# Prompt tiles 1 to 6 in pairs: attention tile by tile, the output stages of both on one stream of weights

## The reference

```
xn = rms_norm(x);  z = xn @ w_in                      # latents, retention q k v, gates
q  = rms_norm(q_lat) @ w_uq ;  q_abs = q_nope . w_uk
o_lat = softmax(q_abs . ckv + q_pe . krope) . ckv     # 8 heads, causal
o_ret = retention over chunks of 128 rows, 4 heads, state carried from chunk to chunk
o_a = (o_lat . w_uv) @ w_oa ;  o_b = (silu(rg) * group_norm(o_ret)) @ w_ob
x  += (sigmoid(ga) * o_a + sigmoid(gb) * o_b) @ w_out
xn2 = rms_norm(x) ;  q = xn2 @ peer_w_q               # 8 heads x 2 halves
s = q . sub_keys ; the best 16 of each half, then the best 16 of their sums: 128 experts a token
y = sum over the 128 experts e of  g_e * gelu(peer_u[e] . xn2) * peer_v[e]
out = rms_norm(x + y)
```

## Time and profile before

| | |
|---|---|
| runs | 4175.75, 4164.13, 4177.30 us |
| the profiled execution, its span | 4170.0 us (the profile gives no other time for it) |
| TensorE busy | 3270.2 us, 78% |
| VectorE busy | 2704.6 us, 65% |
| GpSimd busy | 2494.4 us, 60% |
| ScalarE busy | 739.7 us, 18% |
| 16 DMA engines | 1498.19 MB, mean 359 GB/s |
| mean granted TensorE clock | 0.912 of 2.4 GHz |

### The profile page before, as it was taken

How to read it: one execution, slowest core, us unless ns; L and a number is a source line. 1 busy time by engine, 2 the same in 40 slices (tenths; PEclk the granted TensorE clock), 3 DMA queues, 4 the chain that set the end, 5 groups by cost and what they waited for, 6 DMA issues and landing times.

```text
span 4170.0 us, 39232 instructions
## 1 busy us (share of the span) xinstructions
PE 3270.2 (78%) x11253; PEld 1605.8 (39%) x11253; DVE 2704.6 (65%) x6214; ACT 739.7 (18%) x2273; POOL 2494.4 (60%) x2069
## 2 busy tenths in 40 slices
PE   7877877767888877867988777877898777799854
PEld 3334333332344332423444333433353323466532
DVE  2156568766876578766876577657875686655544
ACT  2112111220112111211121022202131120211111
POOL 0005766777666767776666667666667675544452
PEclk9998999988999999889989999999999997899976
DMA  5668999999999999999999999999999999999996
GB/s 184 219 225 301 402 391 400 353 403 381 398 372 376 403 395 343 365 402 402 384 369 398 402 371 364 382 402 398 390 389 398 397 349 346 327 320 323 327 387 232
DMA packets 580362, 1498.19 MB, mean 359 GB/s; under 512 B 90506, under 2 KB 147475, under 8 KB 580147
## 3 DMA queue, kind: packets, MB, share of 16 engines
q0 software_dynamic: 297216, 1082.26, 67.8%
q1 hardware_dynamic: 242850, 401.10, 26.7%
q10 hardware_dynamic: 40082, 12.32, 1.2%
HBM read 1485.33 MB, written 10.13 MB: 359 GB/s over the span
## 4 chain that ended last, share of the span: by engine, by line
PE 35%; DMA 24%; POOL 16%; issue 11%; DVE 10%; ACT 3%; another core or an unknown queue 1%; ACTq 0%; SPq 0%; DVEq 0%; POOLq 0%
POOL rows L723 15%; DMA rows<-in_peer_v_dram,pe_id 14%; PE PS L1185 12%; PE PS L818 11%; DMA rows<-in_peer_u_dram,pe_id 4%; PE PS L1102 3%; DVE rows L2136 3%; PE PS L827 2%; DMA wbuf<-in_w_in_dram 2%; DMA wbuf<-in_peer_w_q_dram 2%; DMA wbuf<-in_w_out_dram 2%; PE PS L783 1%; DVE xr L2162 1%; PE PS L963 1%
## 5 line engine op out<-in xcount | busy, mean ns | idle before, releaser
L723 POOL DMA_INDIRECT rows<-in_peer_u_dram,pe_id x1024 | 1241.3, 1212 | 919.7 <-PE PS L1185 308.9
L1185 PE MATMUL PS<-rows,diags 128*128 128x512 f32 x2544 | 1357.0, 666 | 457.4 <-DMA rows<-in_peer_v_dram,pe_id 394.8
L723 POOL DMA_INDIRECT rows<-in_peer_v_dram,pe_id x1024 | 1233.8, 1205 | 697.0 <-DVE dots L2136 379.1
L2136 DVE CUSTOM_DVE_ANT_0 rows<-rows,px 128x1024 f32<-128x1024 f32 x1024 | 1242.2, 1223 | 503.0 <-DMA rows<-in_peer_u_dram,pe_id 477.7
L1185 PEld LDWEIGHTS PS<-rows,diags 128*128 128x128 f32 x2544 | 490.8, 208 | 1105.4 <-issue 987.6
L818 PE MATMUL PS<-wbuf,xt 128*128 128x512 f32 (+1 forms) x1696 | 781.1, 597 | 81.4 <-DMA wbuf<-in_w_in_dram 38.3
L2162 DVE SCALAR_TENSOR_TENSOR xr<-rows,gcoef,xr 128x1024 f32<-128x1024 f32 x388 | 498.4, 1285 | 158.9 <-issue 146.5
L818 PEld LDWEIGHTS PS<-wbuf,xt 128*128 128x128 f32 x1696 | 322.1, 197 | 510.4 <-issue 364.2
L818 PE MATMUL PS<-wbuf,wide 128*128 128x512 f32 (+1 forms) x736 | 344.8, 610 | 37.4 <-ACT wide L1292 15.2
L2242 ACT ACTIVATE diags<-ident,gcoef 128x128 f32<-128x128 f32 x636 | 231.1, 399 | 203.7 <-PE PS L1185 81.7
L818 PEld LDWEIGHTS PS<-wbuf,wide 128*128 128x128 f32 x736 | 145.1, 202 | 221.8 <-issue 163.2
(11 more groups left out here) (374 smaller groups left out, 2665.6 us busy)
## 6 DMA issues: line engine op xcount, KB each, us to landing
wbuf<-in_w_in_dram SPq DMA_DIRECT2D x278, 512.0 KB
wbuf<-in_peer_w_q_dram SPq DMA_DIRECT2D x136, 512.0 KB
wbuf<-in_w_out_dram SPq DMA_DIRECT2D x68, 512.0 KB
wbuf<-in_w_ob_dram SPq DMA_DIRECT2D x66, 512.0 KB
wbuf<-in_w_oa_dram SPq DMA_DIRECT2D x36, 512.0 KB
rows<-in_peer_u_dram,pe_id POOLq DMA_INDIRECT x1028, 4.3
rows<-in_peer_v_dram,pe_id POOLq DMA_INDIRECT x1024
KV<-in_cache_ckv_dram SPq DMA_DIRECT2D x128, 128.0 KB
```

The source lines that it names most:

```text
L723: pool.indirect_dma_start(row_slot(kind, n), None, a["peer_u" if kind == "u" else "peer_v"][0], bass.IndirectOffsetOnAxis(ap=pe_id[t % 2][ ...
L1185: last = nc.tensor.matmul(bank[3 + 4 * c], diag(n), row_slot("v", n)[:, c * 512:(c + 1) * 512], start=start, stop=stop)
L2136: V.tensor_tensor_reduce(out=row, in0=row, in1=px[:, :], scale=1.0, scalar=0.0, op0=ALU.mult, op1=ALU.add, accum_out=dots[:, at_:at_ + 1]) ...
```

## The change

The prompt's fronts become *units*: (0), (1, 2), (3, 4), (5, 6), (7). In a unit of two, the attention part of both tiles (lat to heads, and ov) runs one tile after the other. Then rg, oa, gate, ob, out and wq run once for both: every load of 512 KB serves four matmuls of 128x512. linA of a unit's first tile is shared with its second tile (and tile 7's with the sample), nothing else is shared. Loads of blocks fall from 680 to 516. rg and ob no longer stand between heads.

What a pair can't hold goes to four scratch tensors in DRAM: the first tile's retention output (`late_o`) and the second tile's turned input (`late_xt`), back into `z` before rg; the residual and the normed rows of tiles 2, 4, 6 and 7 (`late_x`, `late_px`), back into `xr` and `px` when the expert part of that tile begins. For these tiles a wait on the load stands on VectorE ahead of the first u row (`px_in`) and of the first v row (`late_x_in`), and the load is issued by ScalarE after `u_used` of the tile before. The y rows are stored from ScalarE's queue. pe_id and pg get a third buffer. The page slots of the sample go from 16 to 15.

The turns are dealt by weights: `UNIT_TURNS` gives 0, 64, 128, 128 and 72 turns to the units, the sample gets the other 130, and within a unit each yield's share follows `BESIDE`. On which engine a v row is added follows the stage at which it comes.

```diff
+    UNITS = [(0,), (1, 2), (3, 4), (5, 6), (7,)]
+    PAIRS = [u for u, tiles in enumerate(UNITS) if len(tiles) == 2]
+    unit_of = {t: u for u, tiles in enumerate(UNITS) for t in tiles}
+    LEADS = [tiles[0] for tiles in UNITS] + [T]
+    SHARED = [t for t in range(T) if t not in LEADS] + [T]
+    LATE = [2, 4, 6, 7]
...
+    order = [(0, "linA", range(NA))]
+    for u, tiles in enumerate(UNITS):
+        order += [(t, "uq", range(NU)) for t in tiles]
+        order += [(tiles[0], name, part) for name, part in (("rg", range(2)), ("oa", range(2)), ("gate", range(2)), ("ob", range(2)),
+                                                            ("gate", range(2, 4)), ("out", range(2)), ("wq", range(4)))]
+        order += [(LEADS[u + 1], "linA", range(NA))] if LEADS[u + 1] < T else []
+    order += [(T, name, range(count[name])) for name in ("uq", "rg", "ob", "oa", "gate", "out", "wq")]
...
+        pe_id = [sb(f"pe_id{i}", P, U32) for i in range(3)]
+        pg = [sb(f"pg{i}", P) for i in range(3)]
...
+                    self.oret, self.xt, self.ov = [z0, oret], [xt[:, :], z1], [ovt[:, :], vt_b]
+                    self.rg = [[wk[0], wk[1]], [wide[:, 0:D], wk[3]]]
+                    self.t2, self.oa, self.ob = [wide[:, 0:D], z0], [wk[1], wk[2]], [wk[0], oret]
+                    self.gate = [[WK[:, 3 * D:3 * D + 512], WK[:, 3 * D + 512:4 * D]], [ovt[:, :], vt_b]]
+                    self.res, self.xn2 = [xr[tiles[0] % 2][:, :], wk[0]], [wk[2], wk[1]]
+                    self.x2t, self.pq = [xt[:, :], z1], [wide[:, 0:D], z0]
...
+        late_o = nc.dram_tensor("late_o", [len(PAIRS), P, D], F32, kind="Internal").ap()
+        late_xt = nc.dram_tensor("late_xt", [len(PAIRS), P, D], F32, kind="Internal").ap()
+        late_x = nc.dram_tensor("late_x", [len(LATE), P, D], F32, kind="Internal").ap()
+        late_px = nc.dram_tensor("late_px", [len(LATE), P, D], F32, kind="Internal").ap()
...
+        deals = [dealt(names, UNIT_TURNS[u], lambda i, n: BESIDE[n]) for u, names in enumerate(unit_names)]
+        STEPS = T * NPAIR + LAG
...
+            stage = turn_stage[min((n + LAG) // 2, len(turn_stage) - 1)]
+            on_pe.append(stage in ALL_ON_PE or (stage in MOST_ON_PE and n % 3 > 0) or (stage in HALF_ON_PE and n % 2 == 1))
...
+        def sp_unit(sp, u):
+            tiles, at_ = UNITS[u], places[u]
+            lead, last = tiles[0], tiles[-1]
+            committed.wait(sp, u - 1)
+            for t in tiles:
+                if t == lead:
+                    sp_mask(sp, t)
+                sp_blocks(sp, t, "uq")
+                if t != lead:
+                    max_ready.wait(sp, lead)
+                    sp_mask(sp, t)
...
+            if len(tiles) == 2:
+                k = PAIRS.index(u)
+                DJ.wait_drained(sp, last, "stateU")
+                sp.wait_ge(ckv_stored, 32 * (last + 1))
+                late_o_out.wait(sp, k)
+                sp.dma_start(z0, late_o[k]).then_inc(z_in.sem, 16)
+                late_xt_out.wait(sp, k)
+                sp.dma_start(z1, late_xt[k]).then_inc(z_in.sem, 16)
...
+            if last in LATE:
+                merged.wait(sp, lead)
+                sp_residual(sp, last, at_.res[-1])
+            sp_gain(sp, at_.gain, last)
...
+        def pe_block(pe, tiles, name, i, lhs, banks=None):
+
+            n0, slots = load_at[tiles[0], name, i]
             for n in range(n0, n0 + slots):
                 _, _, _, k0, kn, _, wd = loads[n]
                 block_w = w_place(n)
                 pe.wait_ge(*w_arrived(n))
-                if t == T:
-                    w4 = wd // 4
-                    for j in range(kn):
-                        for q in range(4):
-                            last = nc.tensor.matmul(bnk[32 * q:32 * (q + 1), 0:w4], lhs[:, (k0 + j) * P:(k0 + j) * P + 32],
-                                                    block_w[:, j * wd + q * w4:j * wd + (q + 1) * w4],
-                                                    start=(k0 + j == 0), stop=(n == n0 + slots - 1 and j == kn - 1))
-                for j in range(kn if t < T else 0):
-                    last = nc.tensor.matmul(bnk, lhs[:, (k0 + j) * P:(k0 + j + 1) * P], block_w[:, j * wd:(j + 1) * wd],
-                                            start=(k0 + j == 0), stop=(n == n0 + slots - 1 and j == kn - 1))
-                for j in range(kn if t + 1 == T and other is not None else 0):
-                    w4 = wd // 4
+                for j in range(kn):
+                    for x, t in enumerate(tiles):
+                        if banks is None and k0 + j == 0:
+                            A.may_fill(pe, t, name, i)
+                        b = A.bank(t, name, i) if banks is None else banks[x]
+                        last = nc.tensor.matmul(b[:, 0:wd], lhs[x][:, (k0 + j) * P:(k0 + j + 1) * P], block_w[:, j * wd:(j + 1) * wd],
+                                                start=(k0 + j == 0), stop=(n == n0 + slots - 1 and j == kn - 1))
+                last.then_inc(w_used, 1)
+                yield name
...
+            for h in range(NH):
+                if h + 1 < NH:
+                    scores(h + 1)
+                yield "head"
...
+                if h == 5 and first_of_two:
+                    act.wait_ge(ckv_stored, 32 * (t + 1))
+                    for i in range(NA):
+                        A.wait_drained(act, t, "next linA", i)
+                        b = homes[t + 1][i]
+                        wd = stream[i][3]
+                        act_into(z, i * BW, b if len(b.shape) == 3 else b[:, 0:wd], wd, t + 1).then_inc(taken, 1)
...
+                if t in LATE:
+                    k = LATE.index(t)
+                    act.dma_start(late_px[k], at_.xn2[x]).then_inc(late_out.sem, 16)
+                    act.dma_start(late_x[k], at_.res[x]).then_inc(late_out.sem, 16)
...
+            for x, t in enumerate(tiles):
+                for _ in dve_chosen(dve, t, x):
+                    yield "linA"
+                    if not two:
+                        yield "linA"
+            yield "end"
...
+                    if step % NPAIR == 0 and step // NPAIR in LATE:
+                        px_in.wait(dve, LATE.index(step // NPAIR))
...
+                t, after = divmod(step, NPAIR)
+                if after == 0 and t in LATE:
+                    k = LATE.index(t)
+                    u_used.wait(act, t - 1)
+                    late_out.wait(act, k)
+                    act.dma_start(px[:, :], late_px[k]).then_inc(px_in.sem, 16)
+                if after == LAG + 3 and 0 < t < T:
+                    y_ready.wait(act, t - 1)
+                    act.dma_start(out["y_p"][0][ds((t - 1) * P, P), :], xr[(t - 1) % 2][:, :]).then_inc(y_stored, 16)
+                if after == LAG + 19 and 0 < t and t + 1 in LATE:
+                    k = LATE.index(t + 1)
+                    act.wait_ge(y_stored, 16 * t)
+                    late_out.wait(act, k)
+                    act.dma_start(xr[(t + 1) % 2][:, :], late_x[k]).then_inc(late_x_in.sem, 16)
                 if step % TOPK == 0 and TOPK <= step <= T * NPAIR:
...
+SAMPLE_SHARES = ((14, 22), (65, 66), (32, 42))
+PAGE_SLOTS = 15
...
+UNIT_TURNS = (0, 64, 128, 128, 72)
+BESIDE = {"lat": 1.5, "uq": 1.0, "reto": 1.5, "squares": 1.5, "normed": 1.5, "keys": 1.5, "head": 2.0, "ov": 1.5, "rg": 0.25, "oa": 0.25,
+          "gate": 0.25, "ob": 0.25, "merge": 2.0, "out": 0.25, "x2": 2.0, "wq": 0.3, "pqT": 1.0, "top": 1.0, "xT": 1.0, "linA": 0.4,
+          "end": 0.0}
+ALL_ON_PE = ("lat", "uq", "reto", "squares", "normed", "keys", "ov", "merge", "x2", "pqT", "top", "xT")
+MOST_ON_PE = ("head", "page")
+HALF_ON_PE = ("ret",)
```

More of the change, by code:

```diff
@@ L136, in program @@
     KPS = 2
-    def first(n):
-        return range(count[n])
-    SHARED = {2: {"rg": first("rg"), "gate": first("gate")},
-              4: {"linA": first("linA"), "rg": first("rg"), "gate": range(2)},
-              6: {"linA": first("linA")},
-              T: {"linA": first("linA")}}
-    def shared(t, name, i):
-        return i in SHARED.get(t, {}).get(name, ())
-    def whole(t):
-        return all(shared(t, name, i) for name in ("linA", "rg", "gate") for i in first(name))
-    x_loaded = [t for t in range(T + 1) if not whole(t)]
@@ L154, in program @@
[L154 to L157 removed]
+    assert T == 8
+    UNITS = [(0,), (1, 2), (3, 4), (5, 6), (7,)]
[3 more added lines that the diff above has]
+    SHARED = [t for t in range(T) if t not in LEADS] + [T]
@@ new lines, in sp_unit @@
+            if len(tiles) == 2:
+                k = PAIRS.index(u)
[5 more added lines that the diff above has]
+                sp.dma_start(z1, late_xt[k]).then_inc(z_in.sem, 16)
+            for name, which in (("rg", range(2)), ("oa", range(2)), ("gate", range(2)), ("ob", range(2)), ("gate", range(2, 4))):
+                sp_blocks(sp, lead, name, which)
@@ new lines, in pe_linA @@
+            x_normed.wait(pe, norm_order.index(("own", t)))
+            for i in range(2):
```

(32 more changed lines are left out.)

1808 lines of the change are left out of this document (1033 added, 775 removed).

## The result

The changed kernel takes 4479.24 us (median of 4 runs, 4466.19 to 4491.11), the kernel before beside it 4169.94 us: 1.0747 times as long, 95% interval 1.0715 to 1.0778. The profiled execution has a span of 4464.4 us and a mean granted clock of 0.871 of full speed, against 4170.0 us and 0.912. The forecast was 4184.

What follows compares the result with a forecast made beforehand. Transfers were taken to bound the kernel before, then GpSimd's gathers in the pairs' attention and VectorE at their ends. 322 + 515 + 2 x 903 + 530 + 1005 = 4178 us span, median 4184, range 4040 to 4285.

Steps and rivals of the forecast that it cites:

- TensorE 176 x 0.43 = 76: Pair, rg to x2: TensorE needs 76 us for 176 matmuls, below transfers' 152; the stretch was given 159 us.
- linA of unit (0): Unit (0): linA doubles on TensorE, 48 more matmuls x 0.43 us = 21 us, mostly beside the choice; unit 322 us.
- no engine is busy for 80% of a tile: Reading of the kernel before: no engine reaches 80% of a tile, so transfers set the pace.
- Loads and scratch: Whole kernel: 164 fewer loads save 213 us of DMA time, scratch adds 36, dropped loads save 8; net -185.
- Attention 540 by GpSimd: Pair's attention: 360 rows at GpSimd's 1.50 us make 540 us, against 481 of DMA; bounds 522 and 558.
- Rival 1's full form: Transfers stay the bound everywhere: 3991 us; rival 1, including a form holding in half the stretches (4070), has chance 0.23.
- wq to linA 204: Pair's end: VectorE bounds it at 217 us, less 13 for ring rows fetched ahead, 204; bounds 165 and 240.
- rival 2: Units' ends, wq to linA: gathers lengthen VectorE's chain by 0.26 us each, 75 us, 4259; pair's end over 215; chance 0.25.
- Unit (1, 2) 515: Unit (1, 2): attention 240, rg to x2 112 and the end 163 us sum to 515; bounds 450 and 560.
- Unit (7), 530: Unit (7): attention 240, middle 134, end 148 and 8 for px make 530 us; bounds 500 and 570.
- sample, 1005: Sample's part: 130 turns for 74 add 291 us of transfers, less 6, to 720: 1005 us; bounds 985 and 1030.
- px loads: VectorE's waits for px reloads: nothing for tiles 2, 4, 7 (up to 12 us each without cover), 8 us for tile 6.

Runs made afterwards that it cites:

- e10: Changed kernel with e2's deal, more linA turns and v rows moved, plus every spill written three times (28 more 512 KB writes): 4174.56 us, 1.0064 times the kernel before.
- e6: Changed kernel with gathers of half rows, halving expert-row bytes but not gathers, products or matmuls: 4273.03 us in one run; pair (3, 4) attention 537 us.
- e7: Changed kernel with u products over 512 of 1024 numbers, gathers and bytes unaltered: pair attention 507 us, a gather 1.02 us for 1.12.
- e9: Kernel of e8 with all v rows of the heads added on TensorE: 4090.74 us, 0.9876 times the kernel before.
- e8: Changed kernel with e2's deal, linA and v rows adjusted, and unit (1, 2) turns moved from attention to rg to x2: 4127.47 us, 0.9955 times the kernel before.
- e0: Changed kernel unaltered, timed again on another chip: 4415.26 us, 1.0669 times the kernel before.
- e2: Changed kernel with only the turn weights altered, a pair's attention 73 turns for 90, rg to x2 28 for 17: 4202.96 us, 1.0123 times the kernel before.
- e4: Changed kernel with the v rows of merge and x2 moved from TensorE to VectorE: 4401.89 us, 1.0610 times the kernel before.
- e1: Changed kernel with three quarters of the second tile's shared-block matmuls left out, loads and turns kept: 4293.03 us, 1.0361 times the kernel before.
- e3: Changed kernel with every v row of rg, oa, gate, ob, out and wq added on TensorE: 4537.59 us, 1.0934 times the kernel before.

## Why the prediction was wrong

**The step that failed is "TensorE 176 x 0.43 = 76" in rg to x2.** The text took 0.43 us for a matmul. It is the distance of records, and an fp32 matmul of 128x512 has two. A pair's 44 loads have 352 of them, 151 us; TensorE was busy with them for 153.6. With the v rows and the transposes it is busy for 184 us, more than the 159 given to the stretch, which took 206 with 22 us of TensorE's waits; none was in the sum. The same slip hid the bound of wq: 16 loads x 8 x 0.43 = 55 us, with transposes and v rows 75 of 76. The earlier trace rows held the warning: tile 3's attention has TensorE at 129.80 of 149 us, and the changed kernel does the same matmuls as before (TensorE busy 3261 us, before 3270) on fewer loads. Pairing halves the transfers of a block, not its TensorE time, so the blocks' bound moves from transfers to TensorE. The text weighed DMA, GpSimd and VectorE in every stretch of the pairs, and TensorE in one of them, by the wrong count (linA of unit (0) has the same slip, 21 us for 41, and there it cost nothing: 320 us for 322). That "no engine is busy for 80% of a tile" was a misreading too: the earlier trace rows have TensorE at 357.43 of tile 3's 445 us.

**By its steps:**
- *Loads and scratch.* 1425 MB, as said; q1 is busy 198 us less, near the 213 of the loads alone. That scratch costs 36 us is not borne out: 28 more writes cost 5 to 24 us (e10); the reloads are open.
- *Attention 540 by GpSimd.* Right, 537 and 547; and the reason in the main: half the bytes don't shorten it (e6), shorter products quicken the gathers (e7). In the changed kernel, with no weights but w_uq in this stretch, gathers still start 1.50 us apart; 1.42 of it are the gather and its issue (1.12 + 0.30), the rest mostly waits for a ring place. The rule of the Trainium skill (SBUF — State Buffer, Who interferes with whom), that a VectorE instruction with two SBUF inputs contends with GpSimd's reads of SBUF, agrees with e7: a product at 0.69 us for 1.22 took 0.10 us from each gather. Rival 1's full form is refuted for this deal; in e9, with the share at 0.99 and 1.00 from attention to x2, transfers are at their limit there.
- *wq to linA 204.* Measured 225, past the 215 that rival 2 named. But its mechanism was not it: 76 us of these are wq, bound by TensorE. Top lists and linA are VectorE's (148 of 153 us), and the product's mean there is what the earlier trace rows have: 1221 ns for 1223. The price of 0.26 us a gather on VectorE's side, rival 2's term, is not seen.
- *Unit (1, 2) 515.* Measured 646, the largest single miss. Rg to x2 took 166 for 112, by the same count. The attention took 291 for 240: 20 us pass from the commit to the first product, while VectorE is in the front's first steps and waits; that was in no term. The 160 rows then take 270 us, 1.69 each for the 1.50 of the sum; why is not shown. A further cause is inherent in pairs: this unit has two fronts to run and one tile's experts beside them, so the DMA share is 0.66 and 0.70 in its latter stretches. Its own weights lessen that (e8) and don't remove it (slices 8 and 9 of e9).
- *Unit (7), 530, and sample, 1005.* 547 and 1003. In unit (7) a load has four records, those of one tile, and TensorE is at 105 of 145 us from rg to x2: the slip had no effect there. The sample's 2 us of error are partly luck, for the same part takes 978 to 984 us on the other chips (e0, e2, e4, e8).
- *px loads.* The waits that the trace gives come to 21.9 us at three of the four loads, those of tiles 2, 4 and 7, in stretches that rows bound; tile 6, for which 8 us stood in the sum, is not among them. No wait in rg to x2 names ScalarE's queue.

The range ended at 4285 us. Its ends came from bounds of DMA, GpSimd and VectorE, and so could not hold TensorE's. The slip is not the whole of the miss. Of the 47 us in rg to x2 of pair (3, 4) it accounts for 25 (184 for 159); the other 22 are TensorE's waits, for which the sum had no term.

Of the 286 us between sum and span, rg to x2 of the three shared units holds 54 + 47 + 49 = 150, and wq to linA 26 + 21 + 22 = 69. By e1, e2 and e3 that is TensorE's time together with turns dealt elsewhere. How the 69 divide between TensorE's wq and VectorE's choice, and what of the 51 in the first attention is the wait at its start, was not tried by itself.
